# Two down products and one gate/up product moved ahead of the slot product in a mixture-of-experts stage

## The chip, the core and the metric

The kernel runs on one core of a Trainium2 chip. A core has TensorE (PE, matrix products), VectorE (DVE), ScalarE (ACT), GpSimd (POOL) and SyncE (SP, which here only issues transfers), each with its own instruction stream, and 16 DMA engines that they share. The engines wait for each other through semaphores. The metric is the device time of one execution in microseconds.

## The reference, cut to what matters

Two layers. Each has a mixer and, behind it, a mixture of experts (MoE) that is added to the residual stream:

```python
for i in range(DEPTH):                      # DEPTH = 2
    ...                                     # mixer: MLA attention, then RG-LRU
    x = x + g1[:, None, :] * m
    h = modulate(x, norm_ffn[i], sh2, sc2)
    idx, wts = route(ht, w_router, router_bias)        # 512 tokens, top 2 of 32 experts
    y = moe(ht, idx, wts, moe_w_gu[i], moe_w_dn[i])
    x = x + g2[:, None, :] * y.reshape(B, S, D)

def expert_block(args):                     # D = 1024, D_EXPERT = 512
    xb, e = args
    g, u = jnp.split(xb @ w_gu[e], 2, axis=-1)
    return (jax.nn.silu(g) * u) @ w_dn[e]
```

Everything is float32. An expert has 4 MB of gate/up weights and 2 MB of down weights, 32 experts in each layer.

## The kernel before

**Blocks.** An expert's tokens are handled in blocks of 32 rows. The kernel has a fixed list of NB = 60 blocks for each layer, BLOCKS, numbered here from 0 as in the code; experts that may have many tokens hold 3 to 5 blocks, others 2 or 1. Blocks 0 to 7 belong to the experts 0 to 3, two each; block 8 to the next expert, blocks 9 and 10 to the one after, block 11, blocks 12 to 14, and so on. The order of experts is ORDER, and an expert's place in it is p.

**One block n** takes these steps: rows of the tokens come into xg and are transposed (rows_turned, DVE) into xgT; ACT scales and shifts them (rows_scaled); PE multiplies with the gate/up weights (gate_up, 32 products, which the trace counts as 64); ACT takes the silu; DVE multiplies and transposes (hmid_out); PE multiplies with the down weights (block_down, 16 products, 32 in the trace); DVE scales with the token's weight into yo (down_out). The token's place comes as a one-hot matrix (tokens_hot, DVE).

**Adding to the tokens.** Two blocks, a pair, are put back to their tokens together: combine(p, half) on PE (16 products, 32 in the trace) writes two of four token tiles into PSUM banks 4 to 7, and added(p, half) on DVE adds these to x_tok. Both halves of a pair and all pairs use the same banks, so each combine waits for the added before it (semaphore combine_added). COMBINED says in which block's turn each half stands.

**The turn of a block** on PE in the steady part is: gate_up(n), one combine, block_down(n - 1).

**Start of a layer.** The rows of blocks 0 to 7 are not gathered but picked by matrix products (pick). The weights of the tokens (wtab), their numbers (tok_f) and the indices for the gathers (tok_idx) come from the slot product, slots_products(), whose result DVE turns into these tables. Before it, no down_out, no tokens_hot and no gather can run. POOL gathers the rows of blocks 8 and up from DRAM with indirect transfers. more_set, seven small DVE instructions, counts the blocks beyond the fixed list; more_blocks runs them at block 24 (MORE_BLOCK + 1), where PE is first drained.

**The weights.** Three slots (ring_gu1/ring_dn0, ring_gu0/ring_dn1, arena) hold one expert each. SP issues the transfers in the order of places, in load_expert, gate/up and then down, and each issue waits until the slot's previous expert is through with that product:

```python
sp.wait_ge(S["gu_done"], gone(PREVIOUS[n], l))
sp.dma_start(GU[s]...)
sp.wait_ge(S["dn_done"], gone(PREVIOUS[n], l))
sp.dma_start(DN[s]...)
```

As SP is in order, a down transfer that waits holds up every transfer behind it. For the places that matter here: place 5 (blocks 9, 10) takes the slot of place 2 (blocks 4, 5), so its down transfer waits for block_down(5); place 6 (block 11) takes the slot of place 3 (blocks 6, 7), so its gate/up transfer waits for gate_up(7) and its down transfer for block_down(7); place 7 (blocks 12 to 14) takes the slot of block 8.

The lines of the profile: L1120 pick, L1135 slots_products, L1149 gate_up, L1156 down, L1176 combine (to_tokens) on PE; L2059 rows_turned, L2072 down_out, L2078 and L2083 hmid_out, L2236 to L2244 the tables, L2249 to L2256 more_set, L2294 added, L2303 tokens_hot on DVE; L1549 rows_scaled and L1594 silu on ACT; L607 and L609 the gate/up and down transfers on SP; L727 the gathers on POOL.

## Time and profile before

| | |
|---|---|
| median of 3 runs | 1625.96 us (1624.98 to 1629.66) |
| the profiled execution | 1629.63 us |
| its span in the profile | 1627.9 us |
| PE busy | 1507.0 us (93%) |
| DVE busy | 998.9 us (61%) |
| ACT busy | 591.6 us (36%) |
| POOL busy | 185.9 us (11%) |
| HBM read and written | 497.89 MB and 6.32 MB, 310 GB/s over the span |
| TensorE clock granted, mean | 0.971 of full speed |

The MoE of layer 0 lies at about 385 to 880 us of the span and that of layer 1 at about 1130 us to the end. The profiled execution is one execution, with instructions in order of time; 1.7 us of it lie around the span. In the groups of rows below, a row of the chain or the timeline has its start, its length, the engine, the tile and the line, and how many instructions are merged in it. "issue" in the chain is time in which the engine waited for nothing that the profile shows, and here stands mostly for a wait of PE for weights. In the rows of a stretch, PEclk is the granted clock as a share of full speed (1.00 is 2.4 GHz and 0.50 is 1.2 GHz), then the busy share of the 16 DMA engines and what they moved.

### The profile page before, as it was taken

What the parts mean: (1) busy time and instruction counts of PE and PEld (TensorE: products, weight loads), DVE (VectorE), ACT (ScalarE), POOL (GpSimd) and SP (SyncE); (2) the same over time, 40 slices, a digit from 0 to 9 for tenths busy, and PEclk for the clock granted to TensorE, in tenths of its full rate; (3) what the DMA queues carried; (4) which work ended last, traced back from release to release, by engine and by line L of the source; (5) the groups of instructions that cost most, each with busy time, mean ns of one, the idle gap of its engine ahead of it and who ended that gap; (6) DMA issues with size and microseconds to landing.
All of it is one profiled execution on the core that took longest, in us unless ns stands there. A gap on an engine that the chain in (4) does not pass through costs nothing.

```text
span 1627.9 us, 41680 instructions
## 1 busy us (share of the span) xinstructions
PE 1507.0 (93%) x17987; PEld 880.8 (54%) x17987; DVE 998.9 (61%) x1644; ACT 591.6 (36%) x1526; POOL 185.9 (11%) x216
## 2 busy tenths in 40 slices
PE   3999999998899798999998999997989898999997
PEld 2654455445556455666665444444656555666665
DVE  4677777676565455656555368866666454665655
ACT  2336455124233232333332154534423233333330
POOL 1002112000111011111100122200021110111100
PEclk9999999997999899999999999998989899999999
DMA  9663322399979999999997122029869999999995
GB/s 363 242 250 143 117 78 78 112 335 399 407 306 426 422 423 420 418 422 423 422 428 271 52 78 78 26 94 421 351 248 427 422 422 426 423 422 424 421 425 244
DMA packets 59966, 501.05 MB, mean 308 GB/s; under 512 B 9451, under 2 KB 22268, under 8 KB 43146
## 3 DMA queue, kind: packets, MB, share of 16 engines
q1 hardware_dynamic: 50544, 485.38, 72.8%
q0 software_dynamic: 5088, 7.83, 1.4%
q10 hardware_dynamic: 4154, 5.18, 0.9%
q8 instruction: 144, 2.36, 0.6%
q14 instruction: 36, 0.29, 0.0%
HBM read 497.89 MB, written 6.32 MB: 310 GB/s over the span
## 4 chain that ended last, share of the span: by engine, by line
PE 82%; DVE 7%; DMA 6%; issue 3%; ACT 1%; SPq 0%; DVEq 0%; ACTq 0%
PE ps L1149 25%; PE ps L1176 14%; PE ps L1156 12%; PE ps L1059 7%; DMA ring_gu<-in_w_ada_dram 4%; PE ps L1092 3%; PE ps L1078 3%; PE ps L976 3%; DMA ring_gu<-in_moe_w_gu_dram 2%; PE ps L886 2%; PE ps L996 2%; PE ps L1120 2%; PE ps L950 2%; PE ps L866 2%; PE ps L914 2%
## 5 line engine op out<-in xcount | busy, mean ns | idle before, releaser
L1549 ACT ACTIVATE arena<-arena,shift_col,scale_col 128x32 f32<-128x32 f32 x944 | 299.4, 402 | 69.8 <-DVE arena L2059 69.8
L2294 DVE TENSOR_TENSOR x_tok<-x_tok,ps 128x1024 f32<-128x1024 f32 x236 | 277.9, 1218 | 71.7 <-PE ps L1176 71.2
L1149 PE MATMUL ps<-ring_gu,arena 128*32 128x256 f32 x5120 | 295.1, 382 | 17.5 <-issue 16.7
L1594 ACT ACTIVATE arena<-ps 128x128 f32<-128x128 f32 x120 | 33.2, 277 | 588.5 <-PE ps L1149 588.5
L1149 PEld LDWEIGHTS ps<-ring_gu,arena 128*32 128x32 f32 x5120 | 171.5, 111 | 128.4 <-issue 21.8
L2078 DVE TENSOR_TENSOR arena<-arena,ps 128x128 f32<-128x128 f32 x120 | 34.3, 286 | 301.0 <-ACT arena L1594 301.0
L1176 PE MATMUL ps<-arena 32*128 32x256 f32 x2880 | 201.4, 392 | 10.4 <-DVE arena L2303 8.8
L727 POOL DMA_INDIRECT arena<-xn_dram,tok_idx x104 | 104.4, 1004 | 914.3 <-DVE arena L2059 645.9
L1176 PEld LDWEIGHTS ps<-arena 32*128 32x128 f32 x2880 | 146.9, 189 | 42.6 <-issue 23.1
L1149 PE MATMUL ps<-arena 128*32 128x256 f32 x2560 | 149.9, 387 | 17.0 <-issue 17.0
L1156 PE MATMUL ps<-ring_dn,arena 128*32 128x256 f32 x2560 | 154.2, 382 | 0.9 <-issue 0.9
L1149 PEld LDWEIGHTS ps<-arena 128*32 128x32 f32 x2560 | 85.0, 112 | 75.1 <-issue 22.6
L1156 PEld LDWEIGHTS ps<-ring_dn,arena 128*32 128x32 f32 x2560 | 76.6, 109 | 66.4 <-DVE arena L2083 15.6
L1059 PE MATMUL ps<-arena 128*128 128x512 f32 x256 | 110.6, 592 | 0.2 <-ACT arena L1317 0.2
L1176 PE MATMUL ps<-arena,gate_bc 32*128 32x256 f32 x960 | 81.4, 408 | 12.2 <-DVE arena L2303 5.6
L1059 PEld LDWEIGHTS ps<-arena 128*128 128x128 f32 x256 | 48.6, 190 | 61.1 <-issue 60.7
L1156 PE MATMUL ps<-arena 128*32 128x256 f32 x1280 | 80.5, 392 | 0.0
L2059 DVE STREAM_TRANSPOSE arena<-arena 128x256 f32<-128x256 f32 x104 | 67.5, 649 | 0.0
L976 PE MATMUL ps<-ring_dn 96*128 96x512 f32 x128 | 66.7, 603 | 0.1
L1176 PEld LDWEIGHTS ps<-arena,gate_bc 32*128 32x128 f32 x960 | 45.0, 188 | 37.7 <-issue 30.5
L1842 DVE TENSOR_REDUCE mla_small<-ps 128x1 f32<-128x512 f32 x64 | 44.0, 688 | 25.6 <-PE ps L976 25.4
L1618 DVE SCALAR_TENSOR_TENSOR gate_bc<-ring_gu,c_act,gate_bc 128x1024 f32<-128x1024 f32 x42 | 53.9, 1284 | 8.9 <-DMA ring_gu<-in_w_ada_dram 7.6
(350 smaller groups left out, 1715.3 us busy)
## 6 DMA issues: line engine op xcount, KB each, us to landing
ring_gu<-in_moe_w_gu_dram SPq DMA_DIRECT2D x46, 4096.0 KB
ring_dn<-in_moe_w_dn_dram SPq DMA_DIRECT2D x45, 2048.0 KB
arena<-in_moe_w_gu_dram SPq DMA_DIRECT2D x16, 4096.0 KB
arena<-in_moe_w_dn_dram SPq DMA_DIRECT2D x18, 2048.0 KB
ring_gu<-in_w_ada_dram SPq DMA_DIRECT2D x12, 2048.0 KB, 20.4
ring_gu<-in_w_ada_dram SPq DMA_DIRECT2D x48, 512.0 KB, 4.8
arena<-in_rnn_w_in_dram SPq DMA_DIRECT2D x8, 1024.0 KB, 7.0
arena<-in_moe_w_gu_dram SPq DMA_DIRECT2D x3, 2048.0 KB
```

The lines of the kernel that those rows point to most:

```text
L727: g.indirect_dma_start(xg[:, n % 4, :], None, xn_quarters, bass.IndirectOffsetOnAxis(ap=tok_idx[:, col:col + 1], axis=0), bounds_check=TIL ...
L976: mm(ps[:, 2 + qt, :], qT[0:QK, hb, qt * P:(qt + 1) * P], kT[0:QK, hb, :], start=True, stop=True).then_inc(S["s_ready"], 1)
L1059: last = mm(bank(g), w[:, k, m * P:(m + 1) * P], hT[:, k, :], start=(k == 0), stop=(k == KT - 1))
L1078: last = mm(bank(g), w_rg[:, 2 * mat + k, m * P:(m + 1) * P], xc_[b % 2][:, k, :], start=(k == 0), stop=(k == 1))
L1092: last = mm(bank(g), yT[:, k, i * P:(i + 1) * P], w_o[:, k, hf * HALF:(hf + 1) * HALF], start=(k == 0), stop=(k == KT - 1))
L1149: last = mm(ps[s_ * ROWS:(s_ + 1) * ROWS, pb, 0:2 * QF].rearrange("p (a b) -> p a b", a=2), rows[:, k, :], pair[:, :, s_, :], start=(k == ...
L1156: last = mm(ps[s_ * ROWS:(s_ + 1) * ROWS, pb, 0:QD], src[:, f * ROWS:(f + 1) * ROWS], w[:, f, s_ * QD:(s_ + 1) * QD], start=(f == 0), stop ...
L1176: last = mm(ps[:, bank0 + q, cols * QD:(cols + 1) * QD], hot[part, i * P:(i + 1) * P], rows[part, :], start=(b == 0), stop=(b == len(block ...
L1549: last = A(xgT[:, n % 4, k, :], xgT[:, n % 4, k, :], ACT.Identity, scale=scale_col[:, u, k:k + 1], bias=shift_col[:, u, k:k + 1])
L1618: ins = v.scalar_tensor_tensor(out=acc, in0=w, scalar=ck, in1=acc, op0=ALU.mult, op1=ALU.add)
L2059: v.transpose(xgT[:, n % 4, :, :].rearrange("p k r -> p (k r)"), src.rearrange("p (c k) -> p k c", k=KT)).then_inc(S["rows_turned"], 1)
L2294: return v.tensor_tensor(by_quarter, by_quarter, ps[:, bank0:bank0 + TILES, cols * QD:(cols + 1) * QD], ALU.add)
```

## The change

Before, the turn of block 5 on PE held gate_up(5), the last pick, the slot product, the two halves of pair 0 and block_down(4) between them; from block 6 on every turn had one half of a pair. After, block_down(4) follows the last pick at once, gate_up(6) and block_down(5) come next, and then the slot product. gate_up(7) follows it. The two halves of pair 0 stand in the turn of block 7, those of pair 1 in that of block 8 and those of pair 2 in that of block 9, and from block 10 on the places are those of before. As DVE has no tables yet when block_down(4) and block_down(5) run, block_down(4) writes the second half of its bank's columns (dn_cols), and the waits for yo_ready start at block 6. On ACT, the scaling of block 8's rows stands behind the silu of block 7. DVE's loop is written out for the first blocks to match, with more_set in the turn of block 8 and rows_turned of blocks 8, 9 and 10 in a row.

```diff
@@ -96,8 +96,8 @@
 NCOMB = 2 * NPAIR - 3
 EARLY = TILES + 2
 NPICK = 2 * FIXED
-COMBINED = {n: [((n - TILES) // 2, n % 2)] for n in range(EARLY, NB - 4)}
-COMBINED[EARLY - 1] = [(0, 0), (0, 1)]
+COMBINED = {n: [((n - TILES) // 2, n % 2)] for n in range(EARLY + 4, NB - 4)}
+COMBINED.update({EARLY + 1 + p: [(p, 0), (p, 1)] for p in range(3)})
 COMBINED[NB - 4] = [(NPAIR - 4, 0)]
 COMBINED[NB - 3] = [(NPAIR - 4, 1), (NPAIR - 3, 0)]
 COMBINED[NB - 2] = [(NPAIR - 3, 1)]
@@ -495,6 +495,9 @@
         def dn_bank(n):
             return (3, 6, 7, 4)[n] if n < TILES else (3, 1)[n % 2]
 
+        def dn_cols(n):
+            return slice(QD, 2 * QD) if n == TILES else slice(0, QD)
+
         def gone(place, l):
             return NB * l + LAST[ORDER[place]] + 1
 
@@ -1150,10 +1153,10 @@
                                       rows[:, k, :], pair[:, :, s_, :], start=(k == 0), stop=(k == KT - 1))
                     return last
 
-                def down(pb, src, w):
+                def down(pb, src, w, cols=slice(0, QD)):
                     for f in range(FT):
                         for s_ in range(TILES):
-                            last = mm(ps[s_ * ROWS:(s_ + 1) * ROWS, pb, 0:QD], src[:, f * ROWS:(f + 1) * ROWS],
+                            last = mm(ps[s_ * ROWS:(s_ + 1) * ROWS, pb, cols], src[:, f * ROWS:(f + 1) * ROWS],
                                       w[:, f, s_ * QD:(s_ + 1) * QD], start=(f == 0), stop=(f == FT - 1))
                     return last
 
@@ -1163,11 +1166,11 @@
                     pe.wait_ge(S["hmidT_ready"], base + n + 1)
                     if j == 0:
                         pe.wait_ge(S[f"dn_in{SLOT[place]}"], dn_landed(place, l))
-                    if n >= TILES:
+                    if n >= TILES + 2:
                         pe.wait_ge(S["yo_ready"], base + n - 1)
                     if n == TILES + 1:
                         pe.wait_ge(S["rows_turned"], base + NPICK)
-                    down(dn_bank(n), hmidT[:, n % 2, :], DN[SLOT[place]]).then_inc(S["dn_done"], 1)
+                    down(dn_bank(n), hmidT[:, n % 2, :], DN[SLOT[place]], dn_cols(n)).then_inc(S["dn_done"], 1)
 
                 def to_tokens(bank0, cols, i, blocks):
                     for b, (hot, rows) in enumerate(blocks):
@@ -1238,19 +1241,17 @@
                     gate_up(gu_bank(n), xgT[:, n % 4, :, :], GU[SLOT[place]], range(KT)).then_inc(S["gu_done"], 1)
                     if n == EARLY - 1:
                         pick(NPICK - 1)
-                        slots_products()
+                    if n == EARLY + 1:
                         pe.wait_ge(S["yo_ready"], base + TILES)
-                        pe.wait_ge(S["hmid_ready"], base + n + 1)
-                        combine(0, 0)
-                        block_down(n - 1)
-                        combine(0, 1)
-                        continue
+                        pe.wait_ge(S["hmid_ready"], base + EARLY)
                     for p, half in COMBINED.get(n, []):
                         combine(p, half)
                     if not block_first(n):
                         block_down(n - 1)
                     if n in (TILES - 1, TILES):
                         pick(n + 2)
+                    if n == EARLY:
+                        slots_products()
                 combine(NPAIR - 2, 0)
                 block_down(NB - 1)
                 pe.wait_ge(S["tok_hot_ready"], base + NB)
@@ -1592,7 +1593,9 @@
                     if base + n >= 2:
                         act.wait_ge(S["hmid_ready"], base + n - 1)
                     A(hsil[:, n % 2, :], ps[:, gu_bank(n), 0:QF], ACT.Silu).then_inc(S["sil_ready"], 1)
-                    if n + 2 < NB:
+                    if n == EARLY + 1:
+                        rows_scaled(n + 1)
+                    if n != EARLY and n + 2 < NB:
                         rows_scaled(n + 2)
 
 
@@ -2069,7 +2072,7 @@
                 def down_out(n):
                     col = column(*BLOCKS[n])
                     dve.wait_ge(S["dn_done"], base + n + 1)
-                    v.scalar_tensor_tensor(out=yo[:, n % 4, :], in0=ps[:, dn_bank(n), 0:QD], scalar=wtab[:, col:col + 1],
+                    v.scalar_tensor_tensor(out=yo[:, n % 4, :], in0=ps[:, dn_bank(n), dn_cols(n)], scalar=wtab[:, col:col + 1],
                                            in1=gate_bc[:, 1, l * QD:(l + 1) * QD], op0=ALU.mult, op1=ALU.mult
                                            ).then_inc(S["yo_ready"], 1)
 
@@ -2303,7 +2306,22 @@
                     v.tensor_scalar(tok_hot[n % 4], col_id[:, :], tok_f[:, c_:c_ + 1], None, ALU.is_equal
                                     ).then_inc(S["tok_hot_ready"], 1)
 
-                for n in range(NB):
+                for n in range(TILES):
+                    down_out(n)
+                tokens_hot(0)
+                tokens_hot(1)
+                hmid_out(EARLY)
+                hmid_out(EARLY + 1)
+                added(0, 0)
+                tokens_hot(2)
+                tokens_hot(3)
+                added(0, 1)
+                for n in (TILES, TILES + 1):
+                    down_out(n)
+                    tokens_hot(n)
+                for n in (NPICK, NPICK + 1, NPICK + 2):
+                    rows_turned(n)
+                for n in range(NPICK, NB):
                     if n == MORE_BLOCK + 1:
                         down_out(n - 1)
                         more_blocks()
@@ -2311,21 +2329,18 @@
                         conditioning_set()
                     if n == NB - 1:
                         down_out(n - 1)
-                    if n >= EARLY:
-                        hmid_out(n)
+                    hmid_out(n)
                     for p, half in COMBINED.get(n, []):
                         added(p, half)
-                    if n not in (0, MORE_BLOCK + 1, NB - 1):
+                    if n == NPICK:
+                        down_out(n - 2)
+                        tokens_hot(n - 2)
+                    if n not in (MORE_BLOCK + 1, NB - 1):
                         down_out(n - 1)
-                    if n == TILES:
-                        for early in range(TILES - 1):
-                            tokens_hot(early)
-                    if n == TILES + 1:
+                    tokens_hot(n - 1)
+                    if n == NPICK:
                         more_set()
-                        tokens_hot(n - 2)
-                    if n > TILES:
-                        tokens_hot(n - 1)
-                    if NPICK <= n + 3 < NB and n > TILES:
+                    if n + 3 < NB:
                         rows_turned(n + 3)
                 tokens_hot(NB - 1)
                 added(NPAIR - 2, 0)
```

PE around the slot product of layer 0, before: from the last gate_up ahead of it (block 5, L1149) to block_down(5).

```order
L1149 MATMUL ps<-arena 32x256 x32
L1120 MATMUL ps<-x_tok,gate_bc 32x256 x16
L1135 MATMUL ps<-arena 128x226 x8
L1176 MATMUL ps<-arena 128x256 x16
L1156 MATMUL ps<-arena 32x256 x16
L1176 MATMUL ps<-arena 128x256 x16
L1149 MATMUL ps<-ring_gu,arena 32x256 x32
L1176 MATMUL ps<-arena,gate_bc 128x256 x4
L1176 MATMUL ps<-arena 128x256 x4
L1176 MATMUL ps<-arena,gate_bc 128x256 x4
L1176 MATMUL ps<-arena 128x256 x4
L1156 MATMUL ps<-arena 32x256 x16
```

The same place after the change, from the last pick (L1123) on; lines are three higher, L1138 is the slot product and L1152 gate_up, L1159 down, L1179 combine.

```order
L1123 MATMUL ps<-x_tok,gate_bc 32x256 x16
L1159 MATMUL ps<-arena 32x256 x16
L1152 MATMUL ps<-ring_gu,arena 32x256 x32
L1159 MATMUL ps<-arena 32x256 x16
L1138 MATMUL ps<-arena 128x226 x8
L1152 MATMUL ps<-ring_gu,arena 32x256 x32
L1179 MATMUL ps<-arena 128x256 x32
L1159 MATMUL ps<-ring_dn,arena 32x256 x16
```

Both down products of blocks 4 and 5 and gate_up of block 6 now stand ahead of the slot product, and behind it gate_up of block 7 comes first. The 32 rows of L1179 are both halves of pair 0 in one piece, where before block_down(4) (L1156, between two rows of L1176) stood between them.

DVE behind the slot product of layer 0, before: from the last tokens_hot ahead of the first added (L2303) to the first rows_turned of a gathered block (L2059).

```order
L2303 TENSOR_SCALAR gate_bc<-col_id,mla_big 128x512
L2294 TENSOR_TENSOR x_tok<-x_tok,ps 128x1024 x4
L2072 SCALAR_TENSOR_TENSOR arena<-ps,wtab,gate_bc 128x256
L2249 TENSOR_TENSOR mla_small<-arena,up_e 1x448
L2253 TENSOR_REDUCE more_f<-mla_small 1x14
L2249 TENSOR_TENSOR mla_small<-arena,up_e 1x448
L2253 TENSOR_REDUCE more_f<-mla_small 1x14
L2254 TENSOR_SCALAR more_f<-more_f 1x28
L2255 CAST more_i<-more_f 1x28
L2256 CAST more_i<-arena 1x1
L2303 TENSOR_SCALAR arena<-col_id,mla_big 128x512 x2
L2059 STREAM_TRANSPOSE arena<-arena 128x256
```

The same place after the change, from hmid_out of block 7 to that of block 8 (the last row is its first instruction; L2081 and L2086 are hmid_out, L2297 added, L2075 down_out, L2306 tokens_hot, L2062 rows_turned).

```order
L2081 TENSOR_TENSOR arena<-arena,ps 128x128
L2086 STREAM_TRANSPOSE arena<-arena 128x128
L2297 TENSOR_TENSOR x_tok<-x_tok,ps 128x1024 x2
L2306 TENSOR_SCALAR gate_bc<-col_id,mla_big 128x512
L2306 TENSOR_SCALAR arena<-col_id,mla_big 128x512
L2297 TENSOR_TENSOR x_tok<-x_tok,ps 128x1024 x2
L2075 SCALAR_TENSOR_TENSOR arena<-ps,wtab,gate_bc 128x256
L2306 TENSOR_SCALAR arena<-col_id,mla_big 128x512
L2075 SCALAR_TENSOR_TENSOR arena<-ps,wtab,gate_bc 128x256
L2306 TENSOR_SCALAR arena<-col_id,mla_big 128x512
L2062 STREAM_TRANSPOSE arena<-arena 128x256 x3
L2081 TENSOR_TENSOR arena<-arena,ps 128x128
```

hmid_out of blocks 6 and 7 has come ahead of the first added, more_set has gone from its place ahead of pair 1's tokens_hot to the turn of block 8, and the first gathered rows are turned behind both adds of pair 0 and the down_out and tokens_hot of blocks 4 and 5, three blocks in a row.

## Rows read from the trace of the kernel before

**Rows 1.** Page, busy time: engine, busy us (share of the span), instructions.
```profile
PE 1507.0 (93%) x17987; PEld 880.8 (54%) x17987; DVE 998.9 (61%) x1644; ACT 591.6 (36%) x1526; POOL 185.9 (11%) x216
```

**Rows 2.** Chain of waits, layer 0, 380 to 640 us: start, us, what.
```profile
419.94 1.73 PE ps L1156 x32
...
428.57 3.27 PE ps L1135 x16
...
450.75 3.79 PE ps L1176 x32
454.55 3.03 PE ps L1156 x32
...
461.04 1.94 PE ps L1176 x32
462.97 1.86 PE ps L1156 x32
...
479.35 3.45 PE ps L1149 x64
...
545.80 9.38 issue
...
612.52 4.80 issue
617.32 5.32 PE ps L1149 x64
```

**Rows 3.** Chain of waits, layer 1, 1110 us to the end.
```profile
1174.81 3.27 PE ps L1135 x16
...
1290.96 7.65 issue
...
1356.62 4.06 issue
```

**Rows 4.** Stretches: span:us, busy of PE, PEld, DVE, ACT, POOL; PEclk, DMA share, GB/s.
```profile
450.00:460.00 10.00, 9.25 (x113) 5.68 (x116) 5.89 (x12) 2.54 (x8) 1.12 (x2) 0.66 0.19 43
610.00:620.00 10.00, 5.20 (x74) 2.72 (x72) 3.69 (x5) 1.49 (x5) 1.26 (x2) 0.87 0.99 421
```

**Rows 5.** Timeline of SP, layer 0: start, us to issue, line, what.
```profile
427.05 0.34 SPq L607 DMA_DIRECT2D arena<-in_moe_w_gu_dram  x1
457.79 0.33 SPq L609 DMA_DIRECT2D arena<-in_moe_w_dn_dram  x1
...
472.29 0.33 SPq L609 DMA_DIRECT2D ring_dn<-in_moe_w_dn_dram  x1
```

**Rows 6.** Timeline of SP, layer 1.
```profile
1202.83 0.33 SPq L609 DMA_DIRECT2D arena<-in_moe_w_dn_dram  x1
```

**Rows 7.** Timeline of PE, layer 0; in brackets the idle time ahead and its releaser.
```profile
450.75 1.23 PE L1176 MATMUL ps<-arena,gate_bc 32*128 32x256 f32 x8 [2.79 <-DVE arena L2303]
...
598.85 3.66 PE L1149 MATMUL ps<-ring_gu,arena 128*32 128x256 f32 x64 [3.45 <-issue]
```

**Rows 8.** Timeline of DVE, layer 0, 410 to 500 us.
```profile
432.36 0.28 DVE L2238 SCALAR_TENSOR_TENSOR mla_small<-ps,mla_small 128x113 f32<-128x113 f32 x1
...
433.63 1.65 DVE L2072 SCALAR_TENSOR_TENSOR arena<-ps,wtab,gate_bc 128x256 f32<-128x256 f32 x4
435.20 0.89 DVE L2303 TENSOR_SCALAR arena<-col_id,mla_big 128x512 f32<-128x512 f32 x2
...
439.95 2.35 DVE L2294 TENSOR_TENSOR x_tok<-x_tok,ps 128x1024 f32<-128x1024 f32 x2 [3.47 <-PE ps L1176]
...
458.45 0.66 DVE L2059 STREAM_TRANSPOSE arena<-arena 128x256 f32<-128x256 f32 x1
```

**Rows 9.** Timeline of ACT, layer 0.
```profile
451.58 2.54 ACT L1549 ACTIVATE arena<-arena,shift_col,scale_col 128x32 f32<-128x32 f32 x8 [3.28 <-DVE arena L2059]
```

**Rows 10.** Timeline of POOL, layer 0.
```profile
434.77 1.09 POOL L727 DMA_INDIRECT arena<-xn_dram,tok_idx  x1 [127.75 <-issue]
```

**Rows 11.** DMA queues, 439 to 443 us: packets, MB, share of 16 engines.
```profile
q0 software_dynamic: 46, 0.09, 6.2%
```

## The prediction

> **What bounds the kernel now.** I read the page first: PE is busy for 93% of the span [rows 1]. That says PE, but it is an average over stages, so I took the chain of waits next. In layer 0 it shows PE's steady turn, gate_up 3.45, a combine 1.94, a down 1.86 us, 7.25 together, and in it two waits that PE has for no engine: 9.38 us from 545.80 and 4.80 us from 612.52 [rows 2]. Layer 1 has the same two, 7.65 and 4.06 us [rows 3]. The stretches show why: the DMA engines are at a share of 0.99 and 421 GB/s just where PE waits [rows 4]. So from about 460 us to the second of these waits (the first block of place 15, block 26) the layer is bound by the weights that flow in at 421 GB/s; an expert of 6.29 MB takes 6.29 / 421 = 14.9 us. From there PE runs without a wait of weight to the layer's end.
>
> What sets when that flow starts? The stretch 450 to 460 has a DMA share of 0.19 [rows 4]: the engines ran dry. SP's timeline gives the reason: place 5's gate/up transfer was issued at 427.05, its down transfer at 457.79 only, when block_down(5) was through, and SP is in order. The next down transfer, place 6's, follows block_down(7) at 472.29 [rows 5]. In layer 1 place 5's down was issued at 1202.83 [rows 6]. From 457.79 on the flow does not stop. A layer ends earlier or later by what this restart of the flow moves, and not by the work that PE has got behind it.
>
> **The change, part by part.** All times are counted from the end of the slot product: T = 428.57 + 3.27 = 431.84 before [rows 2], 1174.81 + 3.27 = 1178.08 in layer 1 [rows 3]. The place-5 down transfer was issued at T + 25.95 and T + 24.75.
>
> *Ahead of the slot product* go two downs at 1.73 [rows 2] and one gate_up at 3.45, 6.91 us that stood behind it. Their inputs are there: rows and hmidT of blocks 4 to 6 are made by then, and as place 5's gate/up was in by 450 [rows 4], place 4 before it was in by 440 and place 3, whose blocks 6 and 7 are, by 425, at 10 and 14.9 us each. So the slot product ends at T' = T + 6.91 and delays by as much everything that needs its tables. On the gap before the first combine that is no loss, since the work is taken from behind.
>
> *Behind it*, for the DMA: the place-5 down transfer is now issued before the slot product and follows its gate/up without a gap. Place 6's gate/up waits for gate_up(7), which ends at T' + 4.5, so that too follows at once. The next, place 6's down, waits for block_down(7). The dry stretch is not removed, it moves one expert back, from before place 5's down to before place 6's. The flow restarts earlier by x = (457.79 + 14.9) - I, with I the issue behind block_down(7); the 14.9 us are place 5's down and place 6's gate/up, which no longer stand behind the gap.
>
> *When is block_down(7) through?* After T': DVE has the third table operation done at 432.36 + 0.28 before, that is T + 0.80, now T' + 0.80 [rows 8], and frees bank 0; gate_up(7) takes 3.66 as it does behind a gap at full clock [rows 7], to +4.5. combine(0,0), whose yo and tokens_hot are ready at 433.63 + 1.65 and 435.20 + 0.89 as before [rows 8], that is about +4.3, ends at +6.5. Both halves now stand in a row, so PE waits for added(0,0), 2.35 us [rows 8], to +8.9; combine(0,1) to +10.9; added(0,1) to +13.3; down_out(4), 0.4 (a fourth of 1.65), to +13.7, then block_down(6) beside what follows. gate_up(8) waits for rows that DVE turns only now: tokens_hot(4), down_out(5), tokens_hot(5) at 0.4 each, rows_turned(8) 0.66 [rows 8], to +15.6; ACT's scaling 2.54 [rows 9], to +18.2. Then gate_up(8) 3.66, combine(1,0) 1.94, added 2.35, combine(1,1) 2.05 and block_down(7) 1.86 end at +30.1, and with 0.15 to the issue I = T' + 30.3: 469.05 in layer 0, 1215.3 in layer 1. With that x is 3.6 and 2.4 us.
>
> *The clock.* PE's work from +6.5 to +18.2 is two pieces of 2 us between gaps of 2.4, 2.8 and 2.4. What such gaps do the trace shows: a gap of 2.79 us ahead of 450.75 was followed by a combine of 3.79 instead of 1.94 and a down of 3.03 instead of 1.86, 3.0 us lost, with a granted clock of 0.66 (mean) in that stretch, so at the 1.2 GHz level for most of it; 4.80 us of waiting gave a gate_up of 5.32, 1.9 lost. But 3.45 us ahead of 598.85 gave 3.66, nothing lost [rows 2, 4, 7]. I take 1.9 for gate_up(8), and another 1.2 for the half chance of what else falls under the low clock (combine(0,1), or combine(1,1) with block_down(7)). Then I = T' + 33.4: 472.15 and 1218.4, and x = 0.5 and -0.7. The bounds: no loss at all, x = 3.6 and 2.4; all of it at the low clock, combine(0,1) 1.9, gate_up(8) and combine(1,0) 3.0, the last two 1.4, x = -2.7 and -3.9. I take the middle since gaps as in this pattern are nearest to the one at 450.75.
>
> The rule in the Trainium skill's "TensorE: Matmul & The Clock Gate", "HAM oscillation", is that PE should have no idle gaps beyond a stated length. All gaps of the new order are shorter than that. By it nothing would be lost and both layers would gain, 6.0 us together. The trace speaks against it: the gap ahead of 450.75 was shorter as well, and the low clock came [rows 2, 7].
>
> *The tail.* PE starts gate_up(10) at 479.35 before, T + 47.5 [rows 2]. In the new order the turns of blocks 8 and 9 hold a 2.4 us gap each, for the second half of their pair, and more_set stands in front of the add of pair 2; with the 3.1 for the clock I get T' + 46, T + 53, some 5.5 us later than before, and 6.7 in layer 1. It costs nothing while PE's wait for weights at block 19, 9.38 and 7.65 us, covers it. It is the cover that shrinks: to 4 and 1 us.
>
> The sum: 0.5 - 0.7 = -0.2 us, so 1629.63 for the profiled execution stays 1629.8. That execution is 3.67 us above the median of the runs shown, 1625.96, and the forecast for the median is 1626.0.
>
> **The rivals.**
> *A, the clock holds.* Then x is 3.6 and 2.4 and the time 1626.0 - 6.0 - 0.2 = 1620. For it: the row at 598.85 [rows 7], and that the low clock comes at some gaps and not at others. Against: three gaps within 12 us. Chance 0.17. It is also what the skill's rule above comes to.
> *B, PE takes the bound over.* One mechanism: the moved pairs make PE late by 5.5 and 6.7 us at block 10 (8 and 9 if the clock is low for all of it), and it decides once that is more than the wait at block 19 and then the wait at block 26 (4.80 and 4.06) cover. For it: the cover in layer 1 is 1 us at the first, and each transfer is issued by PE's progress, so a late PE also delays the flow. With the low clock for all, x is -2.7 and -3.9 and the end 6.6 later, 1632.6. Against: 9.38 + 4.80 is far more than 8. Chance 0.15.
> *C, the gathers are late.* Before, the four gathers issued from 434.77 [rows 10] moved 46 packets in the 4 us from 439 under full load [rows 11], about one gather, and the rest when the weights had run dry. Now the weights do not run dry before T' + 22. If each of them takes 4 us, block 10's rows come at T' + 20, and rows_turned(10) stands on DVE ahead of hmid_out(8) and of added(1,0), which is wanted at +23.8. At 4 us there are 3.8 to spare; at 6 us it is 2 to 4 us late in each layer, 1630 to 1634. Chance 0.08.
> *D, PE's filled gap counts in full.* PE stood from T to about T + 4.3 before its first combine, and that time now holds work. Were PE the bound all through, both layers would gain it: 1626.0 - 8.6 = 1617.4. For it: 93% busy [rows 1]. Against: the waits for weights behind it, with the DMA engines at 0.99 [rows 2 to 4], and that the gap comes back as three smaller ones. Chance 0.05. The Trainium skill's "Perfetto Trace Analysis", "Optimization Strategies", sets keeping the matmul engine as busy as possible as the goal; followed here, it would book just this gain. That the change does not do what it says is out: the order of the program shows it.
>
> **How the numbers follow.** The forecast, 1626.0, has 0.55, with its own range 1622.5 to 1629.5. The rest is A 0.17, B 0.15, C 0.08, D 0.05. A change under 0.3%, 4.9 us, can't be told from none. Of A about 0.7 lies beyond that, and all of D, and some of the forecast's low edge: faster 0.20. Of B 0.8, of C 0.6, and a little of the forecast: slower 0.20. Same 0.60. The range reaches to A's and B's times: 1618.5 to 1632.5.
>
> **What would show it.** Right: slot product 6.9 us later in both layers; SP's issue of place 5's down ahead of it; the dry stretch of the DMA moved behind place 6's gate/up, at about T' + 23 to + 33 and shorter by little; PE's combine pairs with 2.4 us between the halves; a low granted clock at gate_up(8); PE's wait at block 19 shrunk to some 4 and 1 us, that at block 26 unchanged. Wrong: gate_up(8) at 3.66 in both layers (A); no wait left at block 26 (B); DVE waiting for a gather ahead of hmid_out(8) (C); or a wait at block 19 that is as long as before.

## The result, and the profile after

The changed kernel takes 1635.04 us (median of 20 runs, 1628.05 to 1640.1), the kernel before 1626.92 in the same comparison: a ratio of 1.0044, 95% interval 1.0033 to 1.0055, so about 7 us slower. The forecast was no change, 1626.0, with 1632.5 as the upper end. The profiled execution took 1635.82 us (span 1634.1); that of before 1629.63, so 6.2 us less. On the profile's page PE's share fell by a point [rows 1]:

```profile
PE 1510.8 (92%) x17987; PEld 881.9 (54%) x17987; DVE 997.5 (61%) x1644; ACT 591.8 (36%) x1526; POOL 185.5 (11%) x216
```

All times below are counted from the end of the slot product, T' = 436.01 in layer 0 (432.68 + 3.33) and 1187.97 in layer 1 (1184.64 + 3.33). Counted from the start of gate_up(0), the slot product starts 6.89 us later than before in layer 0 (45.01 against 38.12 us) and 6.92 us later in layer 1, as the prediction had it; where the layer itself starts in the span differs from execution to execution. The chain of waits of layer 0 (start, us, what) answers to [rows 2]:

```profile
552.73 3.03 issue
555.76 3.66 PE ps L1152 x64
...
585.00 1.29 issue
...
596.03 4.18 issue
600.22 6.09 PE ps L1152 x64
...
615.64 2.22 issue
617.86 5.35 PE ps L1152 x64
```

The wait for weights at block 19 shrank from 9.38 to 3.03 us. In layer 1 the same wait went from 7.65 to 1.15:

```profile
1304.27 3.66 PE L1152 MATMUL ps<-arena 128*32 128x256 f32 x64 [1.15 <-issue]
```

So PE still waits for weights in both layers, and they come later. Counted from the same place in the layer (T before, T' - 6.91 now), block 19 starts 3.3 us later in layer 0 and 2.7 us later in layer 1. SP's timeline, layer 0, then layer 1 (start, us to issue, line, what; L610 is a gate/up, L612 a down transfer), answers to [rows 5, 6]:

```profile
432.95 0.33 SPq L612 DMA_DIRECT2D arena<-in_moe_w_dn_dram  x1
442.65 0.34 SPq L610 DMA_DIRECT2D ring_gu<-in_moe_w_gu_dram  x1
473.79 0.33 SPq L612 DMA_DIRECT2D ring_dn<-in_moe_w_dn_dram  x1
...
1184.92 0.33 SPq L612 DMA_DIRECT2D arena<-in_moe_w_dn_dram  x1
1195.24 0.33 SPq L610 DMA_DIRECT2D ring_gu<-in_moe_w_gu_dram  x1
1222.16 0.33 SPq L612 DMA_DIRECT2D ring_dn<-in_moe_w_dn_dram  x1
```

Place 5's down goes out ahead of the slot product, place 6's gate/up at T' + 6.6 and + 7.3, and place 6's down, the issue I at which the flow restarts, at T' + 37.8 and + 34.2. The forecast had I at + 33.4, with + 36.6 as its worst. The prediction's own formula, with the measured I, gives how much earlier the flow restarts (x; a negative x is later): x = 25.95 + 14.9 - 37.8 - 6.91 = -3.9 us in layer 0 and 24.75 + 14.9 - 34.2 - 6.91 = -1.5 in layer 1, together 5.4 us slower. The profiled execution became 6.2 us slower. The sum fits better than its split: block 19 is 3.3 and 2.7 us later, so in layer 1 about 1.2 us of the lateness are not in the formula.

The stretch from T' - 5 to T' + 60 shows the same as bytes (span:us, busy of PE, PEld, DVE, ACT, POOL; PEclk, DMA share, GB/s). Of before, whose slot product is 6.91 us nearer to the layer's start, I take T + 6.91 for T'. Layer 0 and layer 1 of before:

```profile
433.75:498.75 65.00, 59.13 (x956) 37.72 (x960) 38.79 (x66) 17.19 (x58) 11.27 (x11) 0.92 0.82 340
1179.99:1244.99 65.00, 59.70 (x976) 37.87 (x980) 39.62 (x67) 18.44 (x62) 11.35 (x11) 0.92 0.76 316
```

and of the changed kernel:

```profile
431.01:496.01 65.00, 50.10 (x688) 31.61 (x681) 34.75 (x64) 13.77 (x45) 9.09 (x9) 0.84 0.78 321
1182.97:1247.97 65.00, 51.18 (x722) 32.59 (x712) 35.39 (x64) 13.77 (x45) 9.74 (x10) 0.89 0.75 302
```

33 GB/s less in the two windows' sum (623 against 656) is 33 x 65 / 421 = 5.1 us of the flow at its full rate. PE is 9.0 and 8.5 us less busy there, and of these 17.5 us 6.2 reach the end, since its wait at block 19 gave back the rest.

Where I came from is in PE's timeline (start, us, line, what; in brackets the idle time ahead and its releaser), layer 0:

```profile
436.97 3.66 PE L1152 MATMUL ps<-ring_gu,arena 128*32 128x256 f32 x64 [0.95 <-DVE mla_small L2241]
440.56 2.63 PE L1179 MATMUL ps<-arena 32*128 32x256 f32 x32
447.29 3.79 PE L1179 MATMUL ps<-arena 32*128 32x256 f32 x32 [4.10 <-DVE x_tok L2297]
454.05 2.76 PE L1159 MATMUL ps<-ring_dn,arena 128*32 128x256 f32 x32 [2.96 <-DVE arena L2075]
458.27 5.39 PE L1152 MATMUL ps<-ring_gu,arena 128*32 128x256 f32 x64 [1.46 <-ACT arena L1550]
...
468.07 0.72 PE L1179 MATMUL ps<-arena,gate_bc 32*128 32x256 f32 x8 [2.48 <-DVE x_tok L2297]
...
471.28 2.30 PE L1159 MATMUL ps<-ring_dn,arena 128*32 128x256 f32 x32
...
487.25 3.63 PE L1152 MATMUL ps<-arena 128*32 128x256 f32 x64
```

These are gate_up(7), the halves of pair 0, block_down(6), gate_up(8), the start of combine(1,1), block_down(7) and gate_up(10). DVE, which adds the halves and then turns rows 8 and 9:

```profile
444.88 2.35 DVE L2297 TENSOR_TENSOR x_tok<-x_tok,ps 128x1024 f32<-128x1024 f32 x2 [1.26 <-remote]
...
451.15 2.35 DVE L2297 TENSOR_TENSOR x_tok<-x_tok,ps 128x1024 f32<-128x1024 f32 x2 [3.12 <-PE ps L1179]
...
455.00 1.16 DVE L2062 STREAM_TRANSPOSE arena<-arena 128x256 f32<-128x256 f32 x2
```

And ACT's silu of block 7, with the first and the last of POOL's four gathers:

```profile
442.51 0.28 ACT L1595 ACTIVATE arena<-ps 128x128 f32<-128x128 f32 x1 [11.15 <-remote]
```
```profile
438.95 1.09 POOL L730 DMA_INDIRECT arena<-xn_dram,tok_idx  x1 [132.31 <-issue]
...
442.97 1.00 POOL L730 DMA_INDIRECT arena<-xn_dram,tok_idx  x1 [0.30 <-issue]
```

Look at silu(7). By PE's row gate_up(7) ends at 440.63; ACT starts 1.88 us later, and SP, which waits for the same signal, issues at 442.65. From gate_up(7)'s start to silu(7) it is 5.54 us, in layer 1 6.18 (1188.92 to 1195.10). Elsewhere it is 3.7 (gate_up(9), 473.41 to 477.11) to 4.2 us (steady turns of before, 464.65 to 468.84). The granted clock is 1.00 in all four of these stretches. So here those who wait for PE tell when gate_up(7) was through, and its own row of 3.66 us does not. The row of combine(0,0) behind it does show something: it is 2.63 us long, and 3.25 in layer 1, where other combines take 2.01.

### The profile page after: what moved, and what is told of

It is laid out like the page before. It is cut to its first block, busy times and chain, and to the rows that moved or that the text cites. A ratio compares the mean times of both kernels' runs of the same rounds, so it can differ in the third digit from the quotient of the medians.

```text
span 1634.1 us, 41680 instructions
## 1 busy us (share of the span) xinstructions
PE 1510.8 (92%) x17987; PEld 881.9 (54%) x17987; DVE 997.5 (61%) x1644; ACT 591.8 (36%) x1526; POOL 185.5 (11%) x216
## 4 chain that ended last, share of the span: by engine, by line
PE 81%; DVE 8%; DMA 6%; issue 2%; ACT 2%; SPq 0%; POOL 0%; DVEq 0%; ACTq 0%; POOLq 0%
PE ps L1152 25%; PE ps L1179 13%; PE ps L1159 12%; PE ps L1062 7%; DMA ring_gu<-in_w_ada_dram 4%; PE ps L1095 3%; PE ps L1081 3%; PE ps L979 3%; DMA ring_gu<-in_moe_w_gu_dram 2%; DVE x_tok L2297 2%; PE ps L889 2%; PE ps L999 2%; PE ps L1123 2%; PE ps L953 2%; PE ps L869 2%
## 5 line engine op out<-in xcount | busy, mean ns | idle before, releaser
L1152 PE MATMUL ps<-ring_gu,arena 128*32 128x256 f32 x5120 | 303.5, 390 | 22.5 <-issue 15.7
L2297 DVE TENSOR_TENSOR x_tok<-x_tok,ps 128x1024 f32<-128x1024 f32 x236 | 277.7, 1217 | 76.1 <-PE ps L1179 74.4
L1152 PEld LDWEIGHTS ps<-ring_gu,arena 128*32 128x32 f32 x5120 | 173.8, 113 | 140.2 <-issue 32.1
L1179 PE MATMUL ps<-arena 32*128 32x256 f32 x2880 | 203.7, 396 | 14.7 <-DVE x_tok L2297 14.7
L2081 DVE TENSOR_TENSOR arena<-arena,ps 128x128 f32<-128x128 f32 x120 | 34.3, 286 | 292.3 <-ACT arena L1595 285.9
L1179 PEld LDWEIGHTS ps<-arena 32*128 32x128 f32 x2880 | 147.5, 191 | 48.4 <-issue 23.4
L1159 PE MATMUL ps<-ring_dn,arena 128*32 128x256 f32 x2560 | 158.2, 389 | 6.3 <-DVE arena L2075 5.9
L1152 PE MATMUL ps<-arena 128*32 128x256 f32 x2560 | 145.6, 379 | 4.2 <-issue 4.2
L1159 PEld LDWEIGHTS ps<-ring_dn,arena 128*32 128x32 f32 x2560 | 78.3, 111 | 75.0 <-issue 19.4
L1152 PEld LDWEIGHTS ps<-arena 128*32 128x32 f32 x2560 | 83.5, 110 | 59.4 <-issue 6.3
L1179 PE MATMUL ps<-arena,gate_bc 32*128 32x256 f32 x960 | 79.9, 402 | 11.6 <-DVE x_tok L2297 9.9
L1159 PE MATMUL ps<-arena 128*32 128x256 f32 x1280 | 78.7, 386 | 0.0
L2062 DVE STREAM_TRANSPOSE arena<-arena 128x256 f32<-128x256 f32 x104 | 66.8, 645 | 0.0
L1179 PEld LDWEIGHTS ps<-arena,gate_bc 32*128 32x128 f32 x960 | 44.0, 185 | 36.9 <-issue 24.0
## 6 DMA issues: line engine op xcount, KB each, us to landing
ring_gu<-in_w_ada_dram SPq DMA_DIRECT2D x12, 2048.0 KB, 20.1
```

The lines of the kernel that those rows point to most:

```text
L1152: last = mm(ps[s_ * ROWS:(s_ + 1) * ROWS, pb, 0:2 * QF].rearrange("p (a b) -> p a b", a=2), rows[:, k, :], pair[:, :, s_, :], start=(k == ...
L1159: last = mm(ps[s_ * ROWS:(s_ + 1) * ROWS, pb, cols], src[:, f * ROWS:(f + 1) * ROWS], w[:, f, s_ * QD:(s_ + 1) * QD], start=(f == 0), stop ...
L1179: last = mm(ps[:, bank0 + q, cols * QD:(cols + 1) * QD], hot[part, i * P:(i + 1) * P], rows[part, :], start=(b == 0), stop=(b == len(block ...
L2062: v.transpose(xgT[:, n % 4, :, :].rearrange("p k r -> p (k r)"), src.rearrange("p (c k) -> p k c", k=KT)).then_inc(S["rows_turned"], 1)
L2297: return v.tensor_tensor(by_quarter, by_quarter, ps[:, bank0:bank0 + TILES, cols * QD:(cols + 1) * QD], ALU.add)
```

## The experiments

Ratios are to the kernel before in the same comparison, with 95% intervals. The gain in us against the changed kernel is the difference of ratios times 1627. Theory F: a layer's time is set by when the flow of weights restarts. "..." in a diff marks lines left out.

**e1_swap: place 7's gate/up ahead of place 6's down.**

```diff
-                def load_expert(n):
+                def load_expert(n, held=[]):
...
-                    sp.wait_ge(S["dn_done"], gone(PREVIOUS[n], l))
-                    sp.dma_start(DN[s]...)
+                    held.append((n, s, e))
+                    if n == FIXED + 2:
+                        return
+                    for n_, s_, e_ in held:
+                        sp.wait_ge(S["dn_done"], gone(PREVIOUS[n_], l))
+                        sp.dma_start(DN[s_].rearrange("p k n -> p (k n)"), dn_rows(l, e_)).then_inc(S[f"dn_in{s_}"], 16)
+                    held.clear()
```

> Only SP's order changes: place 7's gate/up transfer, which waits for gate_up(8), is issued ahead of place 6's down, which waits for block_down(7). PE, DVE and ACT do as in the changed kernel. Theory F (the layer's time is set by when the flow of weights restarts): the dry stretch ends about 10 us earlier in layer 0 (T'+27.7 in place of T'+37.8) and 8.4 in layer 1, and the time falls by what PE's waits for weights behind block 18 hold, 4 to 9 us per layer: 1617 to 1627 us. Rival B (PE's own lateness from the pairs is what counts): PE is as late as before at block 10, so 1633 to 1637.

1629.78 us, 1.0017 (1.0004 to 1.0029): 4.4 us faster than the changed kernel, with the programs of PE and DVE as they were. That goes against B and is less than F's range. The transfer behind the gap went out at T' + 25.7 and + 25.8 (+ 27.7 and + 25.8 were expected). Behind it stands place 6's down, at T' + 35.65 and + 34.11, and then place 7's down, which waits for block_down(8): from T' + 45 to T' + 50 the DMA share was 0.37 in layer 0 and 0.01 in layer 1. The dry stretch had been split, not closed.

PE has the same instructions as in the changed kernel, and yet gate_up(8) of layer 0, which took 5.39 us there, took 3.66 here, and 3.66 in e2 too:

```profile
457.63 3.66 PE L1157 MATMUL ps<-ring_gu,arena 128*32 128x256 f32 x64 [0.65 <-ACT arena L1555]
```
```profile
460.70 3.66 PE L1152 MATMUL ps<-ring_gu,arena 128*32 128x256 f32 x64 [0.94 <-ACT arena L1550]
```

So where the low clock falls in these turns differs from execution to execution of the same work, and a single trace's I carries that.

**e2_more_late: more_set from block 8 to block 12.**

```diff
-                    if n == NPICK:
+                    if n == NPICK + 4:
                         more_set()
```

> more_set, 3 us of DVE work that the change put in front of block 9's rows, moves from block 8 to block 12. Nothing before block_down(7) changes. Theory F: place 6's down is issued as before the edit (T'+37.8 and T'+34.2), gate_up(10) comes some 3 us earlier and the time stays, 1634 to 1636 us. Rival B: PE is 3 us less late in each layer, 1629 to 1632.

1635.87 us, 1.0056 (1.0034 to 1.0078): no gain, where B had 3 us or more. PE is earlier at block 10 (T' + 49.0 and + 47.5, against + 51.2 and + 49.3) and the time is not. B, PE's own lateness, is refuted. F holds in the time, but I was not left where it was: it came at T' + 36.0 in layer 0, 1.8 us earlier by the clock alone, and at + 34.5 in layer 1.

**e3_rows_early: rows_turned(8) between the adds of pair 0.**

```diff
                 tokens_hot(3)
+                rows_turned(NPICK)
                 added(0, 1)
```

> rows_turned(8) moves on DVE from behind both adds of pair 0 to between them. Theory F: the gather of block 8 has landed by T'+9, so DVE turns the rows in time it stood idle, gate_up(8) loses its wait (1.46 and 0.68 us) and place 6's down comes 1.5 to 3 us earlier in each layer: 1630 to 1633 us. Rival C (the gathers are late): DVE waits for the gather ahead of added(0,1), which gets later, and the time is 1635 to 1639.

1630.35 us, 1.0016 (1.0002 to 1.003): 4.6 us faster. I fell to T' + 33.4 in both layers. DVE did not wait for the gather ahead of rows_turned(8), so C is refuted as it was put.

**e4_halves: the down between the halves of a pair.**

```diff
-                    if n >= TILES + 2:
+                    if n > TILES + 2:
                         pe.wait_ge(S["yo_ready"], base + n - 1)
...
+                    if EARLY < n < EARLY + 4:
+                        combine(n - EARLY - 1, 0)
+                        block_down(n - 1)
+                        combine(n - EARLY - 1, 1)
+                        continue
```

> In blocks 7, 8 and 9 the down of the block before stands between the two halves of the pair and not behind them. Theory F: PE's wait for the first half's add is filled, block_down(7) no longer stands behind combine(1,1), and place 6's down is issued at T'+27 to +31 instead of +37.8 and +34.2; the time falls by 4 to 6 us per layer, 1622 to 1628 us. Rival (the clock and not the order made the loss): the issue comes at T'+34 or later in layer 0 and the time is above 1631.

The first lines of the edit go with it: block_down(6) no longer waits for down_out(4), which DVE has behind both adds of pair 0.

1624.02 us, 0.9977 (0.9962 to 0.9993): 11 us faster than the changed kernel, and faster than before. I is T' + 30.3 and + 29.9. PE now stands 7.17 us ahead of gate_up(8), for rows:

```profile
457.86 5.88 PE L1152 MATMUL ps<-ring_gu,arena 128*32 128x256 f32 x64 [7.17 <-ACT arena L1555]
```

**e5_slots_first: the slot product ahead of block_down(5).**

```diff
+                    if n == EARLY:
+                        slots_products()
                     for p, half in COMBINED.get(n, []):
                         combine(p, half)
                     if not block_first(n):
                         block_down(n - 1)
-                    if n == EARLY:
-                        slots_products()
```

> The changed kernel with the slot product ahead of block_down(5), which then fills the 0.95 us gap ahead of gate_up(7). The question is why ACT and SP see gate_up(7) done 5.5 us (layer 0) and 6.1 us (layer 1) after its start, where 3.7 is usual. If the gap is the cause, silu(7) follows gate_up(7)'s start by 3.7 us, place 6's down is issued about 3 us earlier and the time is 1629 to 1632 us. If the slot product itself leaves PE slow for what follows it, whatever that is, block_down(5) takes the slow part, gate_up(7) a remainder, and only the 0.95 us of the gap is won: 1632 to 1635 us.

1634.25 us, 1.003 (1.0015 to 1.0045), 2.3 us faster than the changed kernel, with intervals that overlap. The gap is gone and the delay has grown: gate_up(7) at 439.61, silu(7) at 446.76, 7.15 us. The gap was not the cause. That the slot product leaves PE slow fitted this run, and so did something I had not written down: the gathers, issued from 440.88 to 445.90, now lay beside more of gate_up(7). e9 tells the two apart.

**e6_halves_rows: e4 and e3 together** (both diffs above).

> e4_halves and e3_rows_early together. In e4 PE stood 7.17 us ahead of gate_up(8), because its rows are turned behind both adds of pair 0. Theory F: with the rows turned between the adds that wait falls to about 2 to 3 us, place 6's down is issued at T'+24 to +27 (e4: T'+30.3 and +29.9), and each layer ends earlier by what its waits for weights behind block 18 still hold, 2 to 5 us: 1615 to 1621 us. Rival (PE is the bound by now): PE is earlier at block 10 by 4 to 5 us in both layers and all of it counts, 1614. Rival (e4 has used up the gain): 1623 to 1625.

1611.08 us, 0.9894 (0.9873 to 0.9914). PE's wait ahead of gate_up(8) is 1.91 us, I is T' + 23.2 in both layers, and the granted clock of the window is 1.00. The gain over e4, 13.5 us, is more than any of the three expectations. With the gaps shorter no low clock came in this window; in e4 the window's granted clock was 0.95. How much of the gain is the clock's and how much the order's, no run separates.

```profile
432.26:497.26 65.00, 56.74 (x906) 36.70 (x900) 41.58 (x74) 19.02 (x63) 11.09 (x11) 1.00 0.98 408
1169.46:1234.46 65.00, 56.87 (x909) 36.99 (x903) 41.67 (x75) 19.11 (x63) 11.10 (x11) 1.00 0.92 378
```

**e7_all: e6 with the edits of e5, e1 and e2.**

> e6 with the slot product ahead of block_down(5), SP's order of e1 and more_set in block 12. Theory F: the dry stretch of the DMA between place 6's gate/up and what follows nearly goes, since place 7's gate/up can go out behind gate_up(8), at about T'+19; gain over e6 limited by the waits that are left: 1611 to 1619 us. Rival (from here PE's own work sets the end): as e6 to within 1.5 us.

1605.77 us, 0.986 (0.9839 to 0.9881), 22.8 us (1.4%) faster than before, and better than F's range. The flow does not run dry any more, 424 and 403 GB/s:

```profile
433.82:498.82 65.00, 60.18 (x972) 38.20 (x975) 42.34 (x73) 19.14 (x63) 11.07 (x11) 1.00 1.01 424
1168.56:1233.56 65.00, 60.04 (x972) 38.62 (x976) 42.34 (x73) 19.14 (x63) 11.11 (x11) 1.00 0.99 403
```

**e8_before_swap: the edit of e1 on the kernel before.**

> The kernel before with SP's order of e1. In it the flow of weights does not run dry between place 5's down and place 7's gate/up, so by theory F the order of the two transfers is worth nothing here: the time stays within 2 us of the kernel before. If instead the order of the transfers by itself made e1 faster (place 7's gate/up wanted earlier), this kernel is 3 to 5 us faster than before.

1629.11 us, 1.0 (0.9987 to 1.0014): in the kernel before, the order of the two transfers is worth nothing.

**e9_gathers_late: the first gathers wait for gate_up(7).**

```diff
                     if n < NPICK + 4:
                         pool.wait_ge(S["picked"], NPICK * (l + 1))
+                        pool.wait_ge(S["gu_done"], NB * l + EARLY + 2)
```

> The changed kernel with the first gathers held back until gate_up(7) is done. Question: what makes gate_up(7) end 1.8 us (layer 0) and 2.5 us (layer 1) late, though its clock is granted in full? In the traces POOL issues four gathers beside it. Theory G (the gathers slow PE or its signals): silu(7) now follows gate_up(7)'s start by 3.7 us, and place 6's down is issued about 2 us earlier, 1631 to 1634 us. Theory S (the slot product leaves PE slow): silu(7) still follows by 5.5 and 6.1 us, the rows of block 8 come later, and the time is 1635 to 1639 us.

1629.58 us, 1.0017 (0.9999 to 1.0036): 4.4 us faster, though the two intervals overlap a little. gate_up(7) starts as before the edit, at 436.95, and silu(7) follows by 3.71 us, in layer 1 by 3.72. PE, ACT and POOL, one row each:

```profile
436.95 3.66 PE L1153 MATMUL ps<-ring_gu,arena 128*32 128x256 f32 x64 [0.96 <-DVE mla_small L2242]
```
```profile
440.66 0.28 ACT L1596 ACTIVATE arena<-ps 128x128 f32<-128x128 f32 x1 [9.31 <-PE ps L1153]
```
```profile
441.60 1.09 POOL L731 DMA_INDIRECT arena<-xn_dram,tok_idx  x1 [136.00 <-PE ps L1153]
```

Theory S is refuted: the slot product is as it was. The four gathers beside gate_up(7) make it end late. But the gathers then stand beside combine(0,0), and the delay moves there in part: added(0,0) starts 1.07 us behind the end of combine(0,0)'s row, and 0.99 in layer 1, where 0.07 is usual. So of its 2.3 us e9 gives added(0,0) back 1.25 in each layer (T' + 7.63 and + 7.54). I went to T' + 34.2 in layer 0 (3.6 earlier), but to + 36.0 in layer 1 (1.8 later): there gate_up(8), of 3.66 us in the changed kernel, took 5.37 behind a gap of 1.44. So of what e9 shows, the delay of gate_up(7) is certain and the effect on the time is not cleanly its own; beside e1 and e2, whose I is 34.1 to 36.0, e9's is no earlier.

**e10_all_no_swap: e7 without the edit of e1.**

> e7 without SP's changed order. Theory F: SP waits for block_down(7), issued some 5 us behind gate_up(8), so the dry stretch is longer by that; layer 0 of e7 had its wait at block 19 (3.82 us), so part of it counts: 1606 to 1610 us. Rival (from here PE's own work sets the end): as e7, 1605 to 1606.5.

1607.85 us, 0.9871 (0.9847 to 0.9896): within F's range, and not told apart from e7 (0.986).

**e11_tokens_late: e7 with the rows of block 8 ahead of two tokens_hot.**

> e7 with rows_turned(8) ahead of tokens_hot(2) and tokens_hot(3) on DVE. PE's wait of 1.91 us ahead of gate_up(8) falls by 0.9 us if the gather of block 8 has landed by then; everything up to block 10 comes 0.9 earlier, and the time by 0 to 1.8 us: 1604 to 1606. If the gather has not landed, no change.

1606.83 us, 0.9858 (0.9832 to 0.9884): the wait fell to 1.12 us as expected and the time stayed. PE's next wait, ahead of combine(1,1), grew from 1.12 to 2.37 us.

**e12_gathers_held: e7 with the gathers of blocks 9 to 11 held back.**

```diff
                         pool.wait_ge(S["picked"], NPICK * (l + 1))
+                        if n > NPICK:
+                            pool.wait_ge(S["gu_done"], NB * l + EARLY + 2)
```

> e7 with the gathers of blocks 9 to 11 held back until gate_up(7) is done; that of block 8 goes out at once, since its rows are wanted first. In e7 silu(7) followed gate_up(7)'s start by 7.1 us with four gathers issued beside it. Theory G: with one gather beside it silu(7) follows by 4 to 5 us, blocks 7 to 9 come 2 to 3 us earlier, and of that 1 to 4 us in all reach the end, as the wait for weights at block 19 grows in layer 0: 1602 to 1605 us where e7 had 1605.8. Rival (one gather alone makes the whole delay): as e7 within 1.5 us.

1606.25 us, 0.9865 (0.9844 to 0.9887), as e7. silu(7) follows gate_up(7) by 3.71 us (439.62 to 443.33) with one gather beside it, where e7 had 7.1 (438.64 to 445.74) with four. So the first gather alone costs nothing that shows. The row of silu, then the first two gathers:

```profile
443.33 0.28 ACT L1607 ACTIVATE arena<-ps 128x128 f32<-128x128 f32 x1 [8.30 <-PE ps L1159]
```
```profile
440.89 1.09 POOL L737 DMA_INDIRECT arena<-xn_dram,tok_idx  x1 [134.72 <-issue]
444.14 1.02 POOL L737 DMA_INDIRECT arena<-xn_dram,tok_idx  x1 [2.16 <-PE ps L1159]
```

The other gathers run beside combine(0,0), and as in e9 its reader is late, 1.04 us behind the end of its row:

```profile
443.19 2.01 PE L1186 MATMUL ps<-arena 32*128 32x256 f32 x32
```
```profile
446.24 2.35 DVE L2309 TENSOR_TENSOR x_tok<-x_tok,ps 128x1024 f32<-128x1024 f32 x2 [1.80 <-PE ps L1186]
```

The time is where the rival had it, but not for the rival's reason. PE was 1.5 us earlier at block 8 and nothing of it reached the end: in layer 0 the wait at block 19 grew from 3.82 to 4.90 us, with the DMA already at its full rate (425 GB/s).

Side by side: I from T' in each layer, the GB/s of the two windows summed, the change against before that this makes at 421 GB/s, and the measured one (ratio x 1627). Where the slot product stands ahead of block_down(5) (e5, e7, e10 to e12), T' + 1.86 is taken for T', the same place in the layer.

| kernel | I, layer 0, 1 | GB/s | by the flow, us | measured, us |
|---|---|---|---|---|
| before | - | 656 | 0 | 0 |
| changed | 37.8, 34.2 | 623 | +5.1 | +7.2 |
| e2 | 36.0, 34.5 | 648 | +1.2 | +9.1 |
| e5 | 36.9, 33.1 | 628 | +4.3 | +4.9 |
| e3 | 33.4, 33.4 | 666 | -1.5 | +2.6 |
| e9 | 34.2, 36.0 | 640 | +2.5 | +2.8 |
| e1 | two dry stretches | 668 | -1.9 | +2.8 |
| e8 | as before | 675 | -2.9 | 0.0 |
| e4 | 30.3, 29.9 | 708 | -8.0 | -3.7 |
| e6 | 23.2, 23.2 | 786 | -20.1 | -17.2 |
| e10 | 21.1, 21.9 | 810 | -23.8 | -21.0 |
| e11 | no dry stretch | 816 | -24.7 | -23.1 |
| e7 | no dry stretch | 827 | -26.4 | -22.8 |
| e12 | no dry stretch | 831 | -27.0 | -22.0 |

The flow accounts for the large steps and for their order, from changed to e4, e6 and the last four, but not for the order of the kernels between 620 and 680 GB/s or among the last four, where the differences are within the noise of the times and of a single trace. It leaves 0 to 5 us (8 in e2, whose time is known to 3.6 us to either side), all of one sign. Part of that is the reference: the profiled execution of before was 2.7 us above its median, and e8, which takes the same time, moved 675 in place of 656.

## Why the prediction was wrong

**What bounds the layer** was right. The time follows the restart of the flow, not PE's work: e2 moved PE's block 10 and not the time, e1 moved the transfer and did, e8 shows that in the kernel before, where the flow has no gap there, the same order does nothing. The formula for x, fed with the measured I, gives 5.4 of the 6.2 us.

**The cover** came out right partly by luck. The wait at block 19 was forecast to shrink to 4 and 1 us and shrank to 3.03 and 1.15. But PE was forecast to reach block 10 5.5 and 6.7 us later than before, and reached it 10.8 and 10.1 us later (T' + 51.2 and + 49.3 in place of + 46), more than rival B's worst case of 8 and 9. What kept a wait at block 19 is that the weights were later too, by the 3.3 and 2.7 us above. The wait at block 26, forecast unchanged, did not stay: it is 2.22 in layer 0 and gone in layer 1, which was one of the prediction's signs of B. It is no proof of B, since PE still waits 3.32 us for weights at block 23:

```profile
1336.82 6.42 PE L1152 MATMUL ps<-ring_gu,arena 128*32 128x256 f32 x64 [3.32 <-issue]
1352.03 5.35 PE L1152 MATMUL ps<-ring_gu,arena 128*32 128x256 f32 x64 [3.25 <-issue]
```

The rows are blocks 23 and 24. The prediction counted two waits in each layer and left out a third, at block 24, where more_blocks drains PE: 3.45 us before in layer 0 and 3.52 in layer 1, now 4.75 and 3.25. The wait at block 23 is new.

**The step that failed is the time of block_down(7), I = T' + 33.4 with + 36.6 as its end (30.3 + 1.9 + 3.0 + 1.4)**. Of its terms, one was missing and one, the clock, was right on average only.

*"gate_up(7) takes 3.66 as it does behind a gap at full clock", to +4.5.* It was done at + 6.4 and + 7.1, and added(0,0) started at + 8.9 and + 8.8 in place of + 6.5. These 2.3 us in each layer were in no bound. e9 and e12 show the cause of gate_up(7)'s lateness: the change put it where PE had stood idle, beside POOL's four gathers. For the 2.3 us as a whole the cause is shown in part: e9 gives 1.25 of them back, about 0.15 are gate_up(7)'s start at + 0.96 in place of + 0.80, and the rest stays in e9 as the lateness of combine(0,0)'s reader, now that the held gathers run beside combine(0,0). I had priced the gathers for when they land, rival C, and not for what they do to PE beside them.

*The clock, 3.1 us, at most 6.3.* Behind those two steps layer 0 lost 1.85 at combine(0,1) (3.79), 1.7 at gate_up(8) (5.39), 1.3 at combine(1,1) (468.07 to block_down(7) at 471.28, 3.2 with 1.94 the usual) and 0.4 at block_down(7) (2.30): 5.2 us, within the bound but well over its middle. Layer 1 lost 1.7, all at combine(0,1); its gate_up(8) took 3.66 behind a gap of 0.68. In e1 and e2, with the same instructions on PE up to block_down(7), block_down(7)'s signal comes at T' + 35.65 and + 34.11, and at + 36.0 and + 34.5, so by the same subtraction the clock cost 3.1, 1.5, 3.4 and 1.9 us. Over these three kernels and two layers the mean is 2.8 us against the 3.1 forecast: the term was right on average, and the 5.2 of layer 0 is the luck of one execution.

Together: 30.3 + 2.3 + 5.2 = 37.8 and 30.3 + 2.3 + 1.7 = 34.3, the measured issues. So the step that failed is the missing term for gate_up(7) beside the gathers, 2.3 us in each layer, which by the flow is, as an estimate, 4.6 us of the 7.2. In the profiled execution the clock added 2.1 in layer 0 and gave back 1.4 in layer 1 against the 3.1. What makes up the rest of the 7.2 us in the medians is open.

**The rivals.** *A* fell: the low clock came in both layers. The sign that the prediction named for A, gate_up(8) at 3.66 in both layers, came in e1 and would have misled: the loss there was at combine(0,1), 3.44 and 3.60 us. The rule of the Trainium skill's "TensorE: Matmul & The Clock Gate", "HAM oscillation", on which A leaned, asks only that PE have no idle gaps beyond a stated length. The gap ahead of combine(0,1) came out longer than forecast, 4.10 and 3.41 us in place of 2.4, so it is no clear test. But the 2.79 us ahead of 450.75 in the kernel before and the 1.46 us ahead of gate_up(8) here are shorter, and the low clock followed both, so the traces do not agree with it. *B* named nearly the right time, 1632.6, from the same low clock, but with a mechanism that e2 refutes: PE came to block 10 earlier there and the end did not. *C* was refuted as put and half right in its object: DVE waited for no gather, and block 10's rows, the third gather (441.67, 10.24 us to landing in the chain), were in at T' + 15.9, where C had T' + 20. *D* fell. The likeliest case had the right mechanism and no term for work laid beside the gathers; the low edge of x, -2.7 and -3.9, with those 2.3 us in each layer, would have reached 1637 and held the result.

What was left open: what in the gathers delays PE. gate_up(7)'s own row and the granted clock show nothing of it, and no run separated the work on POOL from the packets. Nor do the runs say what decides where the low clock falls; up to gate_up(8) e1 and e2 run the changed kernel's instructions on every engine, so the instructions alone do not.

## What to carry to other kernels

Where a queue of large transfers feeds the work, ask of a reordering first at which instruction the queue next waits, and move that one forward; PE's idle time is only the means. The change filled a gap of PE ahead of the wrong instruction and put pairs in front of the right one. A down between the two halves of a pair, and the rows turned in DVE's idle time, turned the same idea from 0.4% slower into 1.1% faster (e6), and with the edits of e5, e1 and e2 into 1.4% (e7). And work that moves into a hole meets what was running beside the hole: list those neighbours, and read a PE step's end from who waits for it.

## What the runs showed of the hardware

- Gathers beside matmuls: with four indirect DMAs of about 1.0 us each, 1.3 us apart on POOL, gate_up(7) ended 1.8 us (layer 0) and 2.5 us (layer 1) late in the changed kernel and about 3.4 us late in e5 and e7 (7.1 us from start to silu, where 3.7 to 4.2 is usual); with the gathers held back, or only the first beside it, not at all (3.71 us). With the held gathers beside combine(0,0) in e9 and e12, its reader came 1.0 to 1.1 us behind the end of its row, where 0.07 is usual. gate_up(7)'s own row (3.66) and the granted clock of 1.00 do not show the delay; the row of the combine behind it does (2.63 and 3.25 us against 2.01).
- Gaps and the clock: gaps of 1.91 us ahead of gate_up(8) cost nothing in e6, e7, e10 and e12 (3.66 in all, granted clock 1.00); 7.17 ahead of it in e4 gave 5.88 and 5.56; 4.10 and 3.41 ahead of a combine gave 3.79 and 3.64 instead of 2.01; but 1.46 in the changed kernel gave 5.39 and 0.68 gave 3.66. So a gap's own length did not decide. Other gaps stood close ahead of the last two in both layers. With the same instructions, e1 and e2 had 3.66 in layer 0, so the loss at one place varies from execution to execution, and no run tells what decides it.
